# VectorE's order in the seven-product down blocks, and finer steps of weight preparation

## The reference

```python
D_FF = 4 * D_MODEL
...
    h = h + jnp.square(jax.nn.relu(hn @ w_up[l])) @ w_down[l]
...
def sq_relu_mlp(h, w_up, w_down):
    u = jax.nn.relu(h @ w_up)
    return (u * u) @ w_down
```

## Time and profile before

| | |
|---|---|
| median of 3 runs | 2087.07 us |
| the profiled execution, its time | 2082.32 us |
| the profiled execution, its span | 2080.4 us |
| TensorE busy | 1982.6 us, 95% |
| VectorE busy | 1315.7 us, 63% |
| ScalarE busy | 839.5 us, 40% |
| mean granted TensorE clock | 0.989 |

### The profile page before, as it was taken

How to read it: one execution, slowest core, us unless ns; L and a number is a source line. 1 busy time by engine, 2 the same in 40 slices (tenths; PEclk the granted TensorE clock), 3 DMA queues, 4 the chain that set the end, 5 groups by cost and what they waited for, 6 DMA issues and landing times.

```text
span 2080.4 us, 32868 instructions
## 1 busy us (share of the span) xinstructions
PE 1982.6 (95%) x14050; PEld 1678.2 (81%) x14050; DVE 1315.7 (63%) x1777; ACT 839.5 (40%) x1266; POOL 129.4 (6%) x131
## 2 busy tenths in 40 slices
PE   6999888899999999999999999999999999999998
PEld 5877777678888887987988879888887677988887
DVE  5477656556568677646546576858456657685844
ACT  4233533234344334344223443534344644343432
POOL 3054000000000000001000000000002200000000
PEclk9999999999999999999999999999999999999999
DMA  7312300323522332322321223232332112323231
GB/s 233 102 61 70 119 8 10 126 88 95 104 81 81 101 120 64 122 68 82 117 82 41 70 72 121 63 122 73 118 101 85 51 62 64 119 69 122 74 102 41
DMA packets 162993, 182.12 MB, mean 88 GB/s; under 512 B 4789, under 2 KB 152261, under 8 KB 162464
## 3 DMA queue, kind: packets, MB, share of 16 engines
q1 hardware_dynamic: 159808, 168.84, 25.5%
q0 software_dynamic: 3040, 11.18, 2.6%
HBM read 172.66 MB, written 7.34 MB: 87 GB/s over the span
## 4 chain that ended last, share of the span: by engine, by line
PE 81%; DVE 11%; issue 3%; ACT 3%; DMA 1%; SPq 0%; DVEq 0%; ACTq 0%
PE M L1341 17%; PE M L1342 16%; PE M L1343 16%; PE M L1425 9%; PE X L1425 5%; PE X L594 2%; DVE raw_lo L2234 1%; PE M L1402 1%; PE M L1404 1%; PE M L1403 1%; DVE w_lo L2234 1%; PE M L594 1%; DVE w_sum L2223 1%; ACT v L1894 1%; DVE ut L2293 1%
## 5 line engine op out<-in xcount | busy, mean ns | idle before, releaser
L2165 DVE TENSOR_TENSOR w_lo<-raw,w_hi 128x2048 fp32r<-128x2048 f32 x119 | 271.5, 2281 | 118.0 <-ACT w_hi L1822 118.0
L1341 PE MATMUL M<-f,w_hi 128*128 128x512 f32 x768 | 304.5, 396 | 0.0
L1342 PE MATMUL M<-f,w_lo 128*128 128x512 f32 x768 | 303.3, 395 | 0.0
L1343 PE MATMUL M<-f,w_hi 128*128 128x512 f32 x768 | 303.2, 395 | 0.0
L1822 ACT ACTIVATE w_hi<-raw 128x2048 fp32r<-128x2048 f32 x119 | 225.3, 1893 | 178.8 <-PE M L1343 54.9
L1878 ACT ACTIVATE us<-ut 128x512 f32<-128x512 f32 x96 | 60.7, 632 | 294.0 <-DVE ut L2293 294.0
L1341 PEld LDWEIGHTS M<-f,w_hi 128*128 128x128 f32 x768 | 144.3, 188 | 35.0 <-issue 0.7
L1342 PEld LDWEIGHTS M<-f,w_lo 128*128 128x128 f32 x768 | 144.3, 188 | 34.9 <-issue 0.7
L1343 PEld LDWEIGHTS M<-f,w_hi 128*128 128x128 f32 x768 | 144.3, 188 | 34.6
L2293 DVE SCALAR_TENSOR_TENSOR ut<-M,rstd 128x512 f32<-128x512 f32 x96 | 66.0, 688 | 144.5 <-PE M L1343 140.1
L1425 PE MATMUL X<-v,w_hi 128*128 128x256 f32 x576 | 116.1, 290 | 27.3 <-DVE h L2246 23.5
(11 more groups left out here) (535 smaller groups left out, 4756.6 us busy)
## 6 DMA issues: line engine op xcount, KB each, us to landing
raw<-in_w_up_dram SPq DMA_DIRECT2D x48, 1024.0 KB, 5.4
raw<-in_w_down_dram SPq DMA_DIRECT2D x48, 1024.0 KB, 5.5
raw<-in_w_in_dram SPq DMA_DIRECT2D x13, 1024.0 KB, 5.4
raw<-in_a_w_in_dram SPq DMA_DIRECT2D x12, 1024.0 KB, 5.3
h<-in_x_dram SPq DMA_DIRECT2D x16, 256.0 KB, 10.2
raw<-in_w_mk_dram SPq DMA_DIRECT2D x4, 1024.0 KB, 5.3
raw<-in_w_mv_dram SPq DMA_DIRECT2D x4, 1024.0 KB, 5.2
raw<-in_w_out_dram SPq DMA_DIRECT2D x4, 1024.0 KB, 6.9
```

The source lines that it names most:

```text
L1341: mm(dst, wh, xh, start=start, stop=False)
L1342: mm(dst, wl, xh, start=False, stop=False)
L1343: return mm(dst, wh, xl, start=False, stop=stop)
L2165: TTO(w_lo[:, n % 2, :, 0:cols], raw[:, n % 4, :, 0:cols], w_hi[:, n % 2, :, 0:cols].bitcast(f32), ALU.subtract).then_inc(S["w_lo_ready"], 1)
```

## The change

VectorE's `out_part` takes P5 as its first part and the snapshots as its second, and the waits that count `st_ev` (TensorE's before P3, SyncE's before a `raw` buffer is loaded again) are renumbered. In the first down block that part also goes ahead of the whole preparation of the next block. `prepare_first` puts `group_lo(n, 0)` between the second and the third sum; `group_lo` 1 and 2 come ahead of the remaining `out_part`s, and `group_lo` 3 behind P7's. On ScalarE `group_hi(m + 1, 2)` moves ahead of `snap(m, 1)`. No instruction is added or removed.

```diff
@@ SyncE, raw_free
-                    sp.wait_ge(S["st_ev"], 5 * FAST[n - 4] + 1)
+                    sp.wait_ge(S["st_ev"], 5 * FAST[n - 4] + 2)
@@ TensorE, down_fast
-                wait("st_ev", 5 * j + 2)
+                wait("st_ev", 5 * j + 1)
                 product(n, "P3", nth, g, all_)
@@ ScalarE, mlp
                             group_hi(m + 1, 0)
                             snap(m, 0)
                             group_hi(m + 1, 1)
+                            group_hi(m + 1, 2)
                             snap(m, 1)
-                            group_hi(m + 1, 2)
                             group_hi(m + 1, 3)
@@ VectorE: block_sums(n) is now block_sums(n, k), one instruction a call, and
+            def prepare_first(n):
+                block_sums(n, 0)
+                block_sums(n, 1)
+                group_lo(n, 0)
+                block_sums(n, 2)
@@ VectorE, out_part
-                if k == 0:
+                if k == 1:
                     dve.wait_ge(S["st_snap"], 2 * j + 2)
...
-                elif k == 1:
+                elif k == 0:
                     dve.wait_ge(S["st_mm"], 7 * j + PRODUCT_NO["P5"])
@@ VectorE, mlp, up block 3 and down blocks
                         if late:
-                            block_sums(m + 1)
+                            prepare_first(m + 1)
...
                         if late:
-                            for k in range(3):
+                            for k in range(1, 3):
                                 group_lo(m + 1, k)
...
+                            if b == 0:
+                                out_part(m, b, 0)
                             if b < 3:
-                                block_sums(m + 1)
-                                group_lo(m + 1, 0)
+                                prepare_first(m + 1)
+                                group_lo(m + 1, 1)
+                                group_lo(m + 1, 2)
                             else:
                                 lo(m + 1)
-                            for k in range(4):
+                            for k in range(1 if b == 0 else 0, 3):
                                 out_part(m, b, k)
-                                if b < 3 and k < 3:
-                                    group_lo(m + 1, k + 1)
+                            if b < 3:
+                                group_lo(m + 1, 3)
+                            out_part(m, b, 3)
```

More of the change, by code:

```diff
@@ L2215, in resid, with block_sums @@
                 norm_step(i, 7, j, h[:, 7, :], V(wname, woff + 7), lo_, hi_)
-            def block_sums(n):
+            def block_sums(n, k):
                 s_ = w_sum[:, n % 2]
                 x_ = quarters(raw, n).rearrange("p m (q c) -> p q m c", c=P)
[L2221 to L2227, removed]
+                if k == 0:
+                    arrived(dve, n)
+                    slot_free(dve, n)
+                    TTO(s_[:, 0:2], x_[:, 1:3], x_[:, 0:1].to_broadcast([P, 2, 4, P]), ALU.add).then_inc(S["st_sum"], 1)
+                elif k == 1:
+                    dve.wait_ge(S["st_sum"], 3 * FAST[n] + 1)
+                    TTO(s_[:, 2], s_[:, 1], x_[:, 1], ALU.add).then_inc(S["st_sum"], 1)
+                else:
+                    dve.wait_ge(S["st_sum"], 3 * FAST[n] + 2)
+                    TTO(s_[:, 3], s_[:, 2], x_[:, 3], ALU.add).then_inc(S["st_sum"], 1)
+            def prepare_first(n):
[3 more added lines that the diff above has]
+                block_sums(n, 2)
             def group_lo(n, k):
```

## The result

The changed kernel took 2112.64 us (median of 4 runs, 2108.35 to 2121.64), the kernel before 2086.57 us (4 runs, 2082.84 to 2093.29). The ratio is 1.0127, with a 95% interval from 1.0085 to 1.0169: slower, by some 26 us. I had said 2104.7 and at most 2112. The direction and the waits were right; the clock's part of the loss was too small.

A forecast was written before the change was run, and what follows sets the result against it. TensorE, busy 95%, was taken as the bound, with VectorE holding it up in places. Losses of 12.0 (order of work), 0.9 (second block) and 4.7 (clock) made 17.6 us; 2087.07 + 17.6 = 2104.7 us, range 2095 to 2112.

The forecast's parts named there:

- parts 1 to 3: First down block: P5 first, `raw_lo` ahead of up block 3's exit, copy ahead of second snapshot; loses 12.0 us.
- part 4: Second down block: no slack left before P7, 0 to 0.3 us lost a group; taken as 0.9 us.
- part 5: Clock falls behind first down block's waits: six of nine instead of three, 1.56 us each; 4.7 us more.
- part 2's delay: Up block 3: first `raw_lo` ahead of the first exit makes P6 0.58 us later; bounds 0 and 0.61.
- my rival of nine falls: All nine first-down-block waits lower the clock: 9.4 us of clock, 22.3 in all, 2109 us; chance 0.20.

The follow-up runs named there:

- The two swap experiments: Changed kernel with ScalarE's old order, ratio 1.0078; kernel before with only ScalarE's copy put ahead of the second snapshot, ratio 0.9992.
- part 2 alone: Kernel before with only `group_lo(m + 1, 0)` put between the second and third sum in up block 3; ratio 1.0040.
- swap alone: Kernel before with only `group_hi(m + 1, 2)` moved ahead of `snap(m, 1)` on ScalarE; ratio 0.9992.
- ScalarE undone: Changed kernel with ScalarE's old order, the second snapshot ahead of the copy that waits for the second sum; 2101.71 us, ratio 1.0078.
- one addition: Kernel before with one 128x512 addition that leads nowhere ahead of P5's part in each group's first down block; ratio 1.0077.
- part 2 undone: Changed kernel with up block 3 back in the order of before; ratio 1.0123.
- two additions: Kernel before with two 128x512 additions that lead nowhere ahead of P5's part in each group's first down block; ratio 1.0116.
- fast version with swap: Fast version with `group_hi(m + 1, 2)` put ahead of `snap(m, 1)` on ScalarE; 2158.15 us, ratio to the kernel before 1.0352.
- early in the first block only: Kernel before with P5's part moved early in each group's first down block alone, the other blocks keeping its old place; ratio 0.9903.
- change repaired: Changed kernel with ScalarE's old order and P5's part behind the first sum in the second and third down blocks; ratio 0.9887.
- fast version: Kernel before with P5's part behind the first sum in all three down blocks, ScalarE and up block 3 as before; 2052.20 us, ratio 0.9844.

## Why the prediction came out too low

The loss of the span, 26.2 us, by the prediction's parts. These are the profiled executions; the medians of both kernels stand 4.3 us above them, so the difference of the medians is the same.

| | predicted | measured |
|---|---|---|
| parts 1 to 3, order of work | 12.0 | 12.0 |
| part 4, second block | 0.9 | 0 |
| part 5, clock, over the three falls of before | 4.7 | 12.7 |
| outside the nine groups | 0 | 1.5 |

- **Parts 1 to 3** held in their sum, and step by step but for one. P3's wait went. From the group's first sum to P7 are 17.50 us against 13.30, 4.20 more (predicted: 4.19). From P7 to the next block there are 2.87 fewer at full clock. 1.33 us a group, 12.0 us. P7's wait is 3.78 us of idle time, and 3.93 counted as I had done, from when P7 could have started (1339.98 + 1.86) to when it did; I had 3.9. The step that came out otherwise is the pause before P6, where I had 0.8 us: it is 0.35, and the rest of part 2's delay lies ahead of P1's last quarter (0.21 us idle), which needs the last quarter of the activations as well. The 0.09 us for the first step after P3's wait is 0.08 by its own numbers. That VectorE and ScalarE take their lists in order, as I had cited, is what the trace shows: nine copies waited 3.5 us each, and the snapshot behind each, whose product P6 was done some 2.7 us before the copy started, waited too. The two swap experiments confirm that the swap makes P7's wait: it goes with the swap and comes with it.
- **Part 4**: the second block has no wait at all; 0.1 us was too careful.
- **Part 5, the clock, is the step that failed**, in its count and in its price. "I take six of nine, halfway", at "the same 1.56 us" each. Measured are nine of nine, and the 27 matmuls took 48.5 us in sum where 9 x 3.45 = 31.0 would do: 17.4 us, 1.94 each. Less the 4.7 us of before that is 12.7 us, 8.0 more than I took: 4.7 of them by the count, 3.3 by the price. I had the count in my rival of nine falls, but priced them all at 1.56, so that it too ended at 2109. With the measured price, 12.0 + 12.7 and the median's 2087 make 2112.
- The price was wrong because I took the cost of a fall from falls after waits of 2.6 us, and put it on waits half as long again. After those of 2.6 us the clock always came back after the shorter time, at 1.2 to 1.6 us a fall. In the changed kernel it stayed low twice as long in five groups of nine, at 2.2 to 2.4 us each; the four others cost 1.5.
- The page of the Trainium skill behind my rival of nine falls (TensorE: Matmul & The Clock Gate, "HAM oscillation — how this bites in real kernels") describes a fall at each wait between bursts. For waits from 3.2 us on the runs agree, nine of nine in four kernels; for those of 2.6 us they don't, three of nine in the kernel before.
- What the 1.5 us outside the nine groups are stays open. The first group already starts 2.0 us later in the changed kernel, ahead of anything that was changed.

What the executions show of waits and falls, from their profiles (cost: time of the matmuls behind the wait, less the same at full clock):

| kernel | wait, us | falls | of these, low twice as long | us each |
|---|---|---|---|---|
| before | 2.61 | 3 of 9 | 0 | 1.56 |
| part 2 alone | 2.61 | 8 of 9 | 0 | 1.4 |
| swap alone | 2.81 | 3 of 9 | 0 | 1.5 |
| ScalarE undone | 3.10 | 6 of 9 | 1 | 1.7 |
| one addition | 3.22 | 9 of 9 | 5 | 2.1 |
| part 2 undone | 3.78 | 9 of 9 | 6 | 2.2 |
| changed kernel | 3.78 | 9 of 9 | 5 | 1.9 |
| two additions | 3.82 | 9 of 9 | 9 | 2.5 |
| fast version with swap | 3.02 and 2.52 | 24 of 27 | 0 | 1.5 |
| early in the first block only | 0.94 | 0 of 9 | | |
| change repaired | at most 0.60 | 0 of 9 | | |
| fast version | none | 0 of 9 | | |

In all of them a fall costs 1.2 to 1.6 us where the clock comes back after the shorter time, and 2.2 to 2.8 where it stays low twice as long; the last column is the mean of the two kinds.

That a longer wait costs more in clock is shown by the two kernels with additions, which differ from the one before in nothing else. The table counts single executions, but the mean granted clock of every execution bears it out: 0.983 to 0.991 in the 33 of the kernel before that ran beside the experiments, 0.979 to 0.982 in the four with one addition, 0.976 to 0.979 in the four with two. Why waits of 2.5 to 2.8 us are followed by a fall sometimes three times in nine and sometimes nearly always stays open.

What the change missed: the first block's P3 wait was the sign of VectorE's backlog, and P5's part was its only urgent piece. The change moved that piece ahead, but it also tied TensorE's next product to a sum behind it, and left the second block's P5 behind everything. The fast version moves P5's part, in all three blocks, and nothing else.

## What to carry to other kernels

When a step is moved ahead on one engine, look at what stands behind it there, and at which engine's urgent step that holds up: a copy that waits for another engine must not stand ahead of the one step that TensorE needs. A wait that goes in one block has to be followed into the next with the same backlog. And a wait of TensorE is to be priced with the clock behind it: here waits of 3.8 us cost another 1.9 to 2.5 us each on average, and removing those of 2.6 us gave back the waits and the falls behind them.

## What I had not expected of the hardware

Equal waits of 2.61 us lowered the clock in three groups of nine in one execution and in eight of nine in another of nearly the same kernel. And falls come in two sizes. Behind waits of 2.6 and 2.8 us the clock was always back after the shorter time, and a fall cost 1.2 to 1.6 us of matmul time. Behind waits of 3.8 us it mostly stayed low twice as long, for 2.2 to 2.8 us, and in part during the wait itself, as in the group at 1344.1.
